# Norms taken in two halves of the tokens, in a float32 two-block transformer on one core

## The reference

```python
def rms_norm(x, g):
    y = x32 * lax.rsqrt(jnp.mean(x32 * x32, axis=-1, keepdims=True) + EPS)
    return y * g
def layer_norm(x, g, b):
    mu = jnp.mean(xf, -1); xc = xf - mu; var = jnp.mean(xc * xc, -1)
    return xc * lax.rsqrt(var + LN_EPS) * g + b

# first block, layers 0 and 1: attention in layer 0, a Fourier mixer in layer 1
x = x + 0.5 * mx[2] * swiglu(modulate(rms_norm(x, g0), mx[0], mx[1]), w_gu, w_d)
x = x + mx[5] * fourier_mix(modulate(rms_norm(x, g1), mx[3], mx[4]), fourier_w)
x = x + 0.5 * mx[8] * swiglu(modulate(rms_norm(x, g2), mx[6], mx[7]), w_gu, w_d)
# second block, twice
h = layer_norm(x)                       # entry; later the norm after the ffn
proj = h @ w_in                         # convolution, two attentions, gating unit
h = layer_norm(ALPHA * h + mix @ w_out)
h = layer_norm(ALPHA * h + (silu(up_a) * up_b) @ w_down)   # up = conv(h @ w_up)
```

## Time and profile before

| | |
|---|---|
| median of 3 runs | 3704.71 us |
| profiled execution, its own time | 3697.62 us |
| its span | 3695.4 us |
| PE busy | 3490.1 us (94%) |
| DVE busy | 1934.6 us (52%) |
| ACT busy | 1252.0 us (34%) |
| POOL busy | 361.2 us (10%) |

### The profile page before, as it was taken

The page is one execution under the profiler, slowest core; times in us unless marked ns, Lnnn a source line. Parts: engine busy times, 40 slices in busy tenths (PEclk is TensorE's granted clock), DMA queues, the critical chain, the costliest instruction groups (busy, mean ns, idle before and its releaser), DMA issues.

```text
span 3695.4 us, 40300 instructions
## 1 busy us (share of the span) xinstructions
PE 3490.1 (94%) x16978; PEld 2876.7 (78%) x16978; DVE 1934.6 (52%) x2662; ACT 1252.0 (34%) x1778; POOL 361.2 (10%) x204
## 2 busy tenths in 40 slices
PE   2999999899979999999999999989999998999998
PEld 2888888787868888788877888766788876678887
DVE  8434343566655453645344333486564648666464
ACT  4322122344433222322233222324442432445242
POOL 3311001111100000000000000320100033010001
PEclk9999999899999999999999999989999999999998
DMA  5423242010115353535222222210232212013221
GB/s 195 142 80 127 86 141 71 34 35 35 35 57 171 126 195 124 182 127 181 91 74 87 96 98 91 89 64 6 69 103 97 97 66 90 6 52 103 97 97 57
DMA packets 95797, 348.81 MB, mean 94 GB/s; under 512 B 10624, under 2 KB 11136, under 8 KB 95104
## 3 DMA queue, kind: packets, MB, share of 16 engines
q1 hardware_dynamic: 94320, 343.06, 27.6%
q10 hardware_dynamic: 1296, 3.18, 0.2%
HBM read 344.10 MB, written 2.10 MB: 94 GB/s over the span
## 4 chain that ended last, share of the span: by engine, by line
PE 84%; DVE 10%; ACT 4%; issue 1%; POOL 1%; DMA 0%; ACTq 0%; DVEq 0%; POOLq 0%
PE PS L343 83%; DVE CAC L1949 2%; ACT G L1160 1%; DVE ST L1755 1%; PE PS L419 1%; DVE WL L1517 1%; DVE X L1928 1%; DVE PTL L1738 1%; DVE G L1619 0%; ACT WH L971 0%; DVE HL L1627 0%; POOL SM L2243 0%; ACT PTH L1141 0%; DVE X L1925 0%; DVE HL L1933 0%
## 5 line engine op out<-in xcount | busy, mean ns | idle before, releaser
L343 PE MATMUL PS<-HH,WH 128*128 128x512 f32 (+1 forms) x3120 | 1193.6, 383 | 38.0 <-DVE HL L1627 16.9
L343 PE MATMUL PS<-HL,WH 128*128 128x512 f32 (+1 forms) x3120 | 1177.8, 378 | 0.0
L343 PE MATMUL PS<-HH,WL 128*128 128x512 f32 (+1 forms) x3120 | 1173.8, 376 | 0.0
L1517 DVE TENSOR_TENSOR WL<-RAW,WH 128x1024 fp32r<-128x1024 f32 x462 | 584.5, 1271 | 766.9 <-ACT WH L971 766.8
L971 ACT ACTIVATE WH<-RAW 128x1024 fp32r<-128x1024 f32 x496 | 522.4, 1057 | 1140.6 <-PE PS L343 1123.0
L343 PEld LDWEIGHTS PS<-HH,WH 128*128 128x128 f32 x3120 | 594.9, 191 | 155.4 <-DVE HL L1627 19.1
L343 PEld LDWEIGHTS PS<-HL,WH 128*128 128x128 f32 x3120 | 594.5, 191 | 109.5 <-issue 5.5
L343 PEld LDWEIGHTS PS<-HH,WL 128*128 128x128 f32 x3120 | 593.6, 190 | 108.8
L343 PE MATMUL PS<-AH,WH 128*128 128x512 f32 x1392 | 526.7, 378 | 1.7 <-DVE WL L1517 1.7
L343 PE MATMUL PS<-AL,WH 128*128 128x512 f32 x1392 | 524.1, 377 | 0.0
L343 PE MATMUL PS<-AH,WL 128*128 128x512 f32 x1392 | 522.9, 376 | 0.0
(11 more groups left out here) (275 smaller groups left out, 3253.9 us busy)
## 6 DMA issues: line engine op xcount, KB each, us to landing
RAW<-wst SPq DMA_DIRECT2D x640, 512.0 KB, 3.3
X<-xT SPq DMA_DIRECT2D x1, 2048.0 KB, 12.2
out<-X SPq DMA_DIRECT2D x8, 256.0 KB, 2.0
PTF<-cb SPq DMA_DIRECT2D x1, 1024.0 KB, 4.7
Y<-yT SPq DMA_DIRECT2D x1, 1024.0 KB, 7.6
PTF<-cb ACTq DMA_DIRECT2D x1, 1024.0 KB, 4.8
HM<-sg ACTq DMA_DIRECT2D x4, 256.0 KB, 3.7
ROPE<-rope SPq DMA_DIRECT2D x1, 512.0 KB, 4.6
```

The lines of the kernel that those rows point to most:

```text
L343: return e.matmul(o, l, r, start=start, stop=stop)
L1517: e.tensor_tensor(lo, raw_block(s), f32(hi), ALU.subtract).then_inc(*did("dve_done", ("wlo", b)))
```

## The change

For the eight norms f10, fo, f11, m0, c0, m1, c1 and end the work is cut into two halves of 256 tokens, hf 0 and hf 1. Tile 7 of the stage before is made by `lin_last`: all K units for the first 256 tokens, then all again for the second, in two PSUM banks. The sums, roots, reciprocals and spreads of half 0 are put between the units of the second pass (`tail_work`), or behind it (c0, c1, f11); those of half 1 between the units of the next stage. That stage begins with `lin_first`: four tiles in step, all eight k for half 0, then all eight k for half 1, so that the four blocks of weights are all held until the second pass. In the mixer the fourth tile is bg0, which had stood alone. In fo the Fourier groups t = 0, 1 come ahead of t = 2, 3. DVE and ACT make 16 half tiles (k 0 to 7 of half 0, then of half 1; for fo k 0 to 3 of both, then k 4 to 7 of both). The two constant loads that ACT issued behind f11's ffn are issued ahead of it, and the stores at the end are 16 in place of 8.

```diff
+HALVED = ("f10", "fo", "f11", "m0", "c0", "m1", "c1", "end")
+def norm_order(stage):
+    runs = ((0, 4), (4, 8)) if stage == "fo" else ((0, 8),)
+    return [(k, hf) for run in runs for hf in range(2) for k in range(*run)]
...
+        def products(o, u, x, hf, start, stop):
+            s = slice(hf * 256, hf * 256 + 256)
...
+        def lin_last(tile, xs, between):
+            for hf in range(2):
+                bk, prior = take((*name, hf), 256)
+                for k, x in enumerate(xs):
+                    if (hf, k) in between:
+                        between[hf, k]()
+                    m = products(bk[:, 0:256], us[k], x, hf, k == 0, k == len(xs) - 1)
...
+                    if hf and us[k][3]:
+                        steps.append(("wfree", us[k][2]))
...
+        def lin_first(tiles, xs, between):
+            taken = [take(t[0], 512) for t in tiles]
+            us = [[unit(t[1][k]) for t in tiles] for k in range(len(xs))]
+            for hf in range(2):
+                for k, x in enumerate(xs):
...
+        def begin_half(st, hf):
+            if st in NORMS:
+                sums((st, hf), ACC, 2 * hf, 2, ("acc", up, 6), True, False, *read)
+            else:
+                sums(("d", st, hf), ACC, 2 * hf, 2, ("cadd", st, 6), True, False, *read)
+                sums(("v", st, hf), A2t, 2 * hf, 2, ("csq", st, 6), True, False)
+        def spread_half(name, hf, parts):
+            bk, prior = take(("sp", name, hf), 512)
...
+        def head_work(st):
+            return {(0, 1): lambda: (begin_half(st, 1), half_stat(st, 1)), (0, 4): lambda: half_spread(st, 1)}
...
+                            lin_last(tile, axs, tail_work(AFTER[st], (0, 7), (1, 4), (1, 9)))
...
+                order = [(g, t) for a in (0, 2) for g in range(2) for t in (a, a + 1)] if r == 0 else ...
+                for n, (g, t) in enumerate(order):
+                    if r == 0 and n == 1:
+                        begin_half("fo", 1)
+                        half_stat("fo", 1)
+                    if r == 0 and n == 2:
+                        half_spread("fo", 1)
...
+            lin_last(tile(7), fx, tail_work("f11", (0, 5), (1, 4), None))
+            half_spread("f11", 0)
...
+            lin_first([(("b0", l), ...), (("b1", l), ...), (("b2", l), ...), (("bg0", l), ...)], xs, head_work(f"m{l}"))
...
+            lin_last(tile(7), ox, tail_work(f"c{l}", (0, 6), (1, 4), None))
+            half_spread(f"c{l}", 0)
...
# ACT
+        def norm_halves(st):
+            last_square(st, 0)
+            half_root(st, 0)
+            for n, (k, hf) in enumerate(norm_order(st)):
+                    e.activation(hview(k, NX)[0][:, s], src, ACT.Identity, bias=bias)...
+                if n == 1:
+                    last_square(st, 1)
+                if n == (3 if st == "fo" else 4):
+                    half_root(st, 1)
+                if n >= 3 and st != "end":
+                    part(upto[LAST[st]], 1)
+            if st in LNORMS and st != "end":
+                prepare(...)
+                for k in range(8):
+                    q.wait_ge("h", st, k)
+                    e.activation(X(k), X(k), ACT.Identity, bias=v2(LNORMS[st][1], k))...
...
# DVE
+        def norm_halves(st, last):
+            last(0)
+            half_stat(st, 0)
+            for n in range(17):
+                if n < 16:
+                    tile(*order[n])
+                if n and st != "end":
+                    low(*order[n - 1])
+                if n == 1:
+                    last(1)
+                if n == (3 if st == "fo" else 4):
+                    half_stat(st, 1)
+                if n >= 4 and st != "end":
                     part(upto[LAST[st]], 1)
```

More of the change, by code:

```diff
@@ L427, in permute, with sums @@
             mm(bk[:, :], perm, src, True, True).then_inc(*did("pe_done", ("tile", name), *more))
[L429 to L435, removed]
+        def sums(name, src, t0, n, step, first, last, *more):
             q.wait_ge(*step)
             for t in range(n):
-                m = mm(bank["st", name][:, t:t + 1], src[:, t * 128:(t + 1) * 128], mean, start and t == 0, stop and t == n - 1)
-            if stop:
+                m = mm(bank["st", name][:, t:t + 1], src[:, (t0 + t) * 128:(t0 + t + 1) * 128], mean, first and t == 0, last and t == n - 1)
+            if last:
                 more = ("stat", name), *more
@@ L458, in norm @@
-            spread(st, N // 128, None, ("rs", st))
+            if st not in HALVED:
+                for m in range(4, 8) if up == "at" else (7,):
+                    sums(st, G(("sq", up, m)), 0, N // 128, ("sq", up, m), False, m == 7, ("gdone", ("sq", up, m)))
+                spread(st, N // 128, None, ("rs", st))
             return [(*hview(k, N), ("h", st, k), 128) for k in range(8)]
@@ L473, in ffn @@
                         ahead = 1 if wide(st) else 2
-                        lin([t for j in range(ahead) for t in tiles(j)], xs)
+                        if st in HALVED:
+                            lin_first([t for j in range(ahead) for t in tiles(j)], xs, head_work(st))
+                        else:
+                            lin([t for j in range(ahead) for t in tiles(j)], xs)
                     elif f >= ahead:
@@ L722, in fourier_out, with center @@
             lin([tile(m) for m in range(4)], fx)
-            for m in range(4, 8):
-                lin([tile(m)], fx, None, {(6, 0): lambda: squares("f11")} if m == 7 else {})
-        def center(st, m, at):
+            for m in range(4, 7):
+                lin([tile(m)], fx)
+            lin_last(tile(7), fx, tail_work("f11", (0, 5), (1, 4), None))
+            half_spread("f11", 0)
+        def center(st, m):
             def first():
@@ L940, in _ @@
         ffn("f10", norm("f10"))
-        modulation(len(todo))
-        upto["before fo"] = allowed()
+        assert not todo
         xs = norm("fo")
```

446 lines of the change are left out of this document (298 added, 148 removed).

## The result

| | us |
|---|---|
| kernel before, median of 4 runs beside it | 3702.78 (3699.65 to 3705.38) |
| changed kernel, median of 4 runs | 3723.89 (3723.47 to 3725.61) |
| ratio, 95% interval | 1.0058 (1.0041 to 1.0076) |
| profiled executions, their own time | before 3697.62, changed 3724.05 |

The account below looks back on a forecast made before the run. PE, busy 94% of the span, bounds the kernel; only its gaps can win. Terms (-1.7, +5.9, -3.5, +0.5, +3, +2.6, +3, -1.6) sum to +8.2 us: 3713 us median; range 3694 to 3721, forecast's own 3705 to 3720 (0 to +15).

Parts of the forecast that it names:

- two bank waits: In fo, PE stops for the bank freed by the k = 7 half tile and for fc0's emptying: 5.6 and 3.6 us.
- (1): At f10 and f11 products begin with a PE wait of 1 to 2 us; DVE's half ops free it after 0.39 us.
- (4): PE waits in tile 7's first pass for A2t, 2 us at c0.
- (5): The stretch from tile 7 to the first store shrinks by 1.6 us.
- (2): PE's longest new waits: fo, fc0's emptying and k = 7 half tile; c0 and c1, first block's WL, about 3 us.
- (3): At c0, ACT's eight shifts end 2 to 3 us later than before relative to tile 7's start.
- plus 1 for the clock: At c0 and c1, PE goes on 1.9 us later, plus 1 for the clock: +3 us each.
- T: End of tile 7's first pass; at c0 forecast at 2638.3, with lo of h(0) at T+7.05.
- The tail: At c0 and c1, ACT's table load and eight shifts delay the next weight block; PE waits 3.3 us for it.
- m0 +0.5 and m1 +2.6: Mixer norms: ACT's three blocks start at 2378.75 (m0) and 3045.95 (m1); bounds -1.5 to +3 and 0 to +4 us.
- Rival B: The clock falls at every shorter wait; f10, f11, m0, m1, c0, c1 each pay up to 2 us: 3720, chance 0.15.

Follow-up runs that it names:

- e5: Changed kernel with half 0's first sums put later in tile 7, for all eight norms: 3712.19 us, 1.0030 to the kernel before.
- e4: Kernel before with only c0 and c1 taken in halves, mixer with three tiles in step: 3706.91 us, 1.0018.
- e6: Changed kernel with ACT's eight shifts behind each layer norm moved later: 3704.02 us, 1.0010 to the kernel before.
- e2: Changed kernel but with fo's norm whole, as in the kernel before: 3717.12 us, 1.0049 to the kernel before.
- e7: Changed kernel with fo's spreads in banks outside the rotation and its first four Fourier banks emptied within the norm: 3719.27 us, 1.0050 to the kernel before.
- e12: Kernel before with only m0 and m1 in halves, four tiles in step, first sums and ACT's shifts later: 3698.68 us, 0.9987.
- e3: Kernel before with only m0 and m1 taken in halves, four tiles in step: 3708.18 us, 1.0022.
- e8: Kernel before with all norms whole and only the mixer's b0, b1, b2 and bg0 run in step: 3699.62 us, 0.9993.
- e11: Kernel before with only c0 and c1 in halves, first sums and ACT's shifts later: 3700.06 us, 0.9985.
- e9: Kernel before with only f10, f11 and end in halves, first sums later, ACT's shifts later behind the four whole layer norms: 3687.96 us, 0.9954.
- e1: Kernel before with only f10, f11 and end taken in halves: 3687.95 us, 0.9968.

## Why the prediction was wrong

**Right: what each norm trades.** f10 (-1.7, measured -0.9), f11 (-3.5, -3.6), fo (+5.9, +6.8) and end (-1.6, -2.0) were read from the rows, and removing fo's halves or its two bank waits took 6.7 and 6.4 us of it away. The fourth tile in step was rightly held to be nothing. Of the five things to look for, (1) and (4) came as written (1.12 and 1.63 us at f11, 1.88 at c0); (5) was 2.0 in place of 1.6. The stops of (2) came at every place named, in fo at 5.1 and 2.0 us for 5.6 and 3.6, but the two next in length, 4.3 and 4.2 us in the mixers, were not on that list; (3) failed, as follows.

**Wrong: "plus 1 for the clock" at c0 and c1 (+3 each, measured +5.4).** The wait for A2t was forecast at 2.1 us and lasted 1.88, but I let it cost its length only. Behind it the clock went to 0.74 and 0.83, so the second pass, half 0's sums and the path to DVE's first half tile ran late: the first product of c0 starts 8.2 us behind DVE's addition of half 0, which itself starts some 0.2 behind T, and forecast was T+7.05. ACT's block behind the shifts came 6.6 us later than before (2677.74 against 2668.83, less the 2.3 by which the kernel was behind), forecast 2 to 3. e5, which shortens just this wait (to 0.36 us), gives 3.3 us at each: 1.5 are the wait, and about as much the clock (over 40 us of c0 it is 0.91 in e5 and 0.87 here; 0.04 of 40 us are 1.6). The size of this miss rests on the profiled executions: in the medians of e4, c0 and c1 alone cost 2.9 us each, as forecast. The tail was named rightly: PE's stop for WL was shorter than forecast (1.6 for 3.3) only because PE itself came later. e6 gives another 1.9 there.

**Wrong: m0 +0.5 and m1 +2.6 (measured +4.5 and +10.4).** I took PE's time at the sums of squares as ACT's time, and priced the lateness of ACT's blocks only. m0's blocks started at 2380.81; forecast was 2378.75, 2379.2 with the 0.4 by which the changed kernel was behind at m0's start. What I had not seen is that PE would stop there for 4.3 us, where before it was 1.0, and what that does: PE is busy 0.39 of 4 us and then runs 8 us at 0.50, the lower level (1.2 GHz). m1 had in addition the wait for POOL's sum in tile 7 (L2559, 1.5 us), whose effect on the products behind it I had left out as at c0: e5 gives 3.5 us at m1. e6 gives 4.1 and 5.6. 2.3 us of m1 lie where DVE works on the convolution: a DVE copy (L2202) met a POOL block there, in all six traces of kernels that halve all eight norms; without fo's halves, in e2, the same copy ran 0.08 us ahead of POOL. First the changed kernel, then e2:

```profile
3125.49 2.34 POOL L2482 TENSOR_TENSOR WL<-RAW,WH 128x1024 fp32r<-128x1024 f32 x1 [0.18 <-ACT WH L1112]
3125.75 2.35 DVE L2202 COPY G<-SM 128x512 f32<-128x512 f32 x1 [0.62 <-POOL SM L2500]
```

```profile
3118.16 0.43 DVE L2355 COPY G<-SM 128x512 f32<-128x512 f32 x1 [0.28 <-POOL SM L2656]
3118.24 2.56 POOL L2638 TENSOR_TENSOR WL<-RAW,WH 128x1024 fp32r<-128x1024 f32 x1 [0.18 <-ACT WH L1150]
```

**The account.** Over forecast, between the first traces: c0 and c1 2.4 each, m0 4.0, m1 7.8, the softmax steps 2.2, fo 0.9, f10 0.8; under it: 1.9 in the stages up to f01 and 0.4 in f11 and end. Together these are the 18.2 us between +8.2 and +26.4. In the medians the miss is 13 us, since before's first trace was one of its quicker runs; against its third trace (span 3700.7) the changed kernel is 21.1 us behind, as the medians have it. Stage by stage against that trace fo is +5.2, m0 +2.9, c0 +3.6, m1 +9.7 and c1 +5.3: the misses of m1 and c1 stand against either trace, while 1.6 to 1.8 us of m0's and c0's are within what before itself varies. The range was too narrow for its own terms as well: their bounds add up to -6 and +19, not 0 and +15. Rival B was the nearest in number (3720, chance 0.15), and the clock did fall behind the shorter waits at c0 and c1. But it is not most of the price: about half of what e5 gives back at c0, and 1.6 of c0's 5.4 us against the first trace of before (0.87 for 0.91 over 40 us, below). Nor does it fall at every shorter wait: at f10 it held.

**Same code, other clock.** Why c0 costs 5.4 us in the changed kernel and 8.4 in e7 can be read from the granted clock. PE's three waits there are the same in both (2.3, 1.9 and 1.6 us), and the clock over c0's 40 us is 0.87 in one and 0.79 in the other: 0.08 of 40 us are 3.2 us, and measured are 3.0. In order, before, its third trace, the changed kernel, e5 and e7:

```profile
2628.00:2668.00 40.00, 36.34 (x169) 30.38 (x168) 27.04 (x39) 17.13 (x26) 5.24 (x4) 0.91 0.12 40
```

```profile
2628.00:2668.00 40.00, 36.34 (x161) 30.42 (x161) 29.61 (x43) 16.18 (x24) 7.29 (x5) 0.83 0.13 44
```

```profile
2630.00:2670.00 40.00, 35.84 (x241) 34.55 (x240) 29.68 (x65) 14.04 (x26) 5.56 (x4) 0.87 0.12 41
```

```profile
2625.00:2665.00 40.00, 37.37 (x251) 35.50 (x250) 32.84 (x69) 16.96 (x30) 7.30 (x5) 0.91 0.17 54
```

```profile
2628.00:2668.00 40.00, 35.83 (x223) 34.85 (x222) 26.91 (x61) 12.31 (x23) 3.84 (x3) 0.79 0.12 41
```

The third trace of before, at 0.83 for 0.91 with the same waits as the first, took 1.8 us more, and not 3.2: part of the stretch at the lower clock lies in the gap, where PE waits for lo. For the softmax steps, the length times what the clock lacks of 1 is 15.4 us in the longest and 8.9 in the shortest of the four shown: 6.5 of the 7.8 us between them.

**Open.** What decides when the clock falls, and so which of these times a stage takes, is not settled. The first two traces of before reach f10 0.3 us apart and agree stage by stage to 0.1 us, and the third, 1.1 us earlier, does not. But the time since the kernel's start does not decide by itself: e12 reaches f10 0.2 us from the first trace and yet shows, in code that is the same up to m0, the third one's +1.6 at fo and -1.3 at f11, and so do e3, e4, e8 and e11, from 2.8 us early to 2.7 late. No run set the moment of arrival by itself. The Trainium skill, "TensorE: Matmul & The Clock Gate", section "What's actually happening", says that the monitor behind the clock runs on its own and is not restarted when a kernel begins, so that where a change of level falls depends on where the work lands. These traces agree with that as far as they go; none of them shows the monitor itself.

## What to carry to other kernels

Price a new wait of PE by what its products do behind it: here 1.5 us less of waiting inside a run of products gave 3.3 us, and moving the work behind a stop of 4.3 us, which had been 1.0, gave 4 to 6. Before work is cut in halves, look at what the helper engines do behind the last half: moving ACT's eight shifts changed nothing in the medians while the norms before them were whole (e9 against e1), and gave 20 us once they were halved (in the profiles 13.5 in the four stages and 9 in the softmax steps, less 2.9 ahead of f10). With two other repairs this turned a loss of 0.6% into a gain of 0.4%; halving only f10, f11 and end gives 0.3 to 0.5%, so the other five halves bring nothing that these runs show. Take several traces of the kernel before: its second repeated the first, and its third was 5.3 us longer.

## What the runs showed of the hardware

- Two executions of before, and two of the changed kernel, agree stage for stage behind f01 within 0.1 us; a third of before ended 5.3 us behind the first. A saving early in the program (e7: 6.4 us) was lost in its profiled execution in later stages that did not change; in the medians 4.6 us of it stayed.
- With the same code and the same waits of PE, c0 took 3.0 us more where the granted clock over 40 us was 0.79 and not 0.87.
- The softmax steps, 543 products with PE waiting between them, took 110.6 to 118.4 us at mean clocks of 0.92 to 0.87, with DVE and ACT busy the same 74 and 48 us.
- A 512-column copy on DVE took 2.35 us when it started 0.26 us behind POOL's 2.34, and 0.43 when it started 0.08 us ahead of POOL's.
